# Expert rows 0 to 196 in pairs: two steps of the main program ahead of two gelus, more adds on VectorE, low parts two gathers later

## What is computed

```python
def swiglu_ffn(h, w_in, w_out):
    gate, up = jnp.split(h @ w_in, 2, axis=-1)
    return (jax.nn.silu(gate) * up) @ w_out

# PEER, for a block of 128 tokens: 8 heads x 16 experts = 128 experts for each token
experts = jnp.take_along_axis(cand_i, pos, axis=-1)
gates = jax.nn.softmax(top_s, axis=-1)
u = expert_down[experts]
vv = expert_up[experts]
act = jax.nn.gelu(jnp.einsum("thkd,td->thk", u, hb), approximate=False)
return jnp.einsum("thk,thkd->td", (gates * act), vv)
```

## Time and profile before

| | |
|---|---|
| median of three runs | 3392.49 us |
| the profiled execution, its time | 3392.38 us |
| its span on the core | 3390.6 us |
| TensorE, VectorE, ScalarE, GpSimd busy | 87%, 64%, 44%, 23% |
| DMA | 833 MB, mean 246 GB/s |
| table loads of ScalarE | 222, 284.8 us |
| gathers | 512, 536.9 MB |

### The profile page before, as it was taken

One profiled execution on the slowest core, in us unless ns is written; L12 is line 12 of the kernel. 1 busy time (PEld: TensorE's weight loads), 2 busy tenths in 40 slices (PEclk: granted clock), 3 DMA queues, 4 the chain that ended last, 5 costly groups with the idle time before them and its releaser, 6 DMA issues.

```text
span 3390.6 us, 38246 instructions
## 1 busy us (share of the span) xinstructions
PE 2964.8 (87%) x13622; PEld 2137.2 (63%) x13622; DVE 2184.4 (64%) x3979; ACT 1507.6 (44%) x2991; POOL 771.4 (23%) x629
## 2 busy tenths in 40 slices
PE   6989999899998899888979998799896777777777
PEld 5868888688776699767868786377673232223222
DVE  7655443586776576255487885877689589655555
ACT  3243222444665444572245556984333333333333
POOL 0000000000111000000027873212333444434432
PEclk8999999999998899999989999899997999999999
DMA  6544444243213387320449999776887999999997
GB/s 245 186 142 136 137 146 142 90 150 119 69 63 104 116 263 257 113 88 12 148 165 343 370 370 359 293 280 236 331 343 310 421 421 421 421 422 422 421 421 331
DMA packets 156925, 833.13 MB, mean 246 GB/s; under 512 B 17344, under 2 KB 19520, under 8 KB 91072
## 3 DMA queue, kind: packets, MB, share of 16 engines
q0 software_dynamic: 73728, 536.90, 39.5%
q1 hardware_dynamic: 79056, 286.30, 25.3%
q10 hardware_dynamic: 3952, 7.48, 0.6%
HBM read 828.52 MB, written 2.10 MB: 245 GB/s over the span
## 4 chain that ended last, share of the span: by engine, by line
PE 52%; DMA 19%; DVE 14%; ACT 9%; issue 4%; POOL 1%; DVEq 0%; SPq 0%; POOLq 0%; ACTq 0%
PE psum L153 51%; DMA tail<-in_experts,tail 19%; ACT L164 4%; DVE tail L187 3%; ACT arena L164 2%; DVE tail L170 2%; ACT tail L164 2%; DVE tail L182 1%; DVE arena L182 1%; DVE rounded L170 1%; DVE region L170 1%; DVE tail L193 1%; POOL tail L216 1%; DVE tail L190 1%; ACT region L164 1%
## 5 line engine op out<-in xcount | busy, mean ns | idle before, releaser
L153 PE MATMUL psum<-tail,arena 128*128 128x256 f32 (+2 forms) x3572 | 1266.8, 500 | 256.5 <-ACT arena L164 240.3
L153 PE MATMUL psum<-rounded,rounded 128*128 128x512 f32 (+1 forms) x7080 | 1332.0, 348 | 57.9 <-DVE rounded L182 41.0
L153 PEld LDWEIGHTS psum<-rounded,rounded 128*128 128x128 f32 x7080 | 1128.4, 191 | 245.1 <-issue 68.6
L153 PEld LDWEIGHTS psum<-tail,arena 128*128 128x128 f32 x3572 | 662.9, 197 | 779.8 <-issue 718.7
L216 POOL DMA_INDIRECT tail<-in_experts,tail x512 | 581.7, 1136 | 1395.9 <-PE psum L153 722.3
L187 DVE CUSTOM_DVE_ANT_0 tail<-tail 128x1024 f32<-128x1024 f32 x512 | 645.1, 1267 | 342.5 <-DMA tail<-in_experts,tail 339.5
L164 ACT ACTIVATE tail<-tail 128x1 f32<-128x1 f32 (+1 forms) x1056 | 267.4, 253 | 783.0 <-DVE tail L187 754.7
L164 ACT ACTIVATE rounded<-arena 128x1024 fp32r<-128x1024 f32 (+3 forms) x389 | 362.5, 949 | 383.4 <-PE psum L153 157.8
L170 DVE TENSOR_TENSOR rounded<-arena,rounded 128x1024 fp32r<-128x1024 f32 (+2 forms) x286 | 321.7, 1125 | 272.5 <-ACT rounded L164 272.2
L164 ACT ACT_TABLE_LOAD x222 | 284.8, 1283 | 14.8 <-PE psum L153 8.7
L164 ACT ACTIVATE arena<-psum 128x256 f32<-128x256 f32 (+1 forms) x210 | 97.3, 480 | 327.9 <-PE psum L153 323.8
(11 more groups left out here) (88 smaller groups left out, 1601.7 us busy)
## 6 DMA issues: line engine op xcount, KB each, us to landing
arena<-in_ada SPq DMA_DIRECT2D x136, 512.0 KB
arena<-in_fin SPq DMA_DIRECT2D x132, 512.0 KB
arena<-in_fout SPq DMA_DIRECT2D x60, 512.0 KB
arena<-in_win SPq DMA_DIRECT2D x56, 512.0 KB
arena<-in_mxbc SPq DMA_DIRECT2D x32, 512.0 KB
arena<-in_pq SPq DMA_DIRECT2D x32, 512.0 KB
arena<-in_ain SPq DMA_DIRECT2D x24, 512.0 KB
arena<-in_mz SPq DMA_DIRECT2D x16, 512.0 KB
```

Of the source, the lines that this page charges most:

```text
L153: return self.e.matmul(o, a, b, start=start, stop=stop, skip_group_check=skip)
```

## The change

Rows 0 to 195 are taken in turns of two, (0, 1), (2, 3), ..., and rows from 196 on one by one. In a turn TensorE makes the step of the first row, the add of the first row of the turn before, the step of the second and the add of the second row before. ScalarE makes both steps, then both gelus, then both diagonals; from row 196 on the gelu stands ahead of the step as before. VectorE makes both dots, then the adds of the turn before, then both steps. `own_add` takes two in three of rows 0 to 67, from row 0 on, where it took one in four from row 17 on; from row 68 to 71 it takes one in two. `pool_low` for piece n stands behind gather n + 2. For block 1 `dve_finish` comes behind the steps.

```diff
+        TOGETHER, APART = 68, 196
...
-            return 16 <= s < 124 and s % (4 if n < 72 else 2 if n < 192 else 8 if n < 256 else 16) == 1
+            if n < TOGETHER:
+                return s % 3 > 0
+            return 16 <= s < 124 and s % (2 if n < 192 else 8 if n < 256 else 16) == 1
...
-                if 3 <= n < len(HALF):
-                    pool_low(e, SPLIT[AGAIN + n])
+                if 5 <= n < len(HALF) + 2:
+                    pool_low(e, SPLIT[AGAIN + n - 2])
...
+        TURNS = [(g,) for g in range(0)]
+        TURNS += [(g, g + 1) for g in range(0, APART, 2)]
+        TURNS += [(g,) for g in range(APART, 512)]
+
         def pe_experts(e):
             main = both(pe_half(e, 1), pe_main(e, 1))
             before_rows(main, iter(()))
...
+            behind = []
+            for rows in TURNS:
+                for g in rows:
+                    c, grp = ALL_GROUPS[g]
...
+                    steps_of(c, grp, main, ranks)
+                    if grp % 2:
+                        next(late, None)
+                    for m in behind[0:1] if g < rows[-1] else behind:
+                        pe_add(e, *ALL_GROUPS[m])
+                    behind = behind[1:] if g < rows[-1] else []
+                if rows[0] and rows[0] % 128 == 0:
+                    pe_finish(e, rows[0] // 128 - 1)
+                behind = list(rows)
+            pe_add(e, *ALL_GROUPS[511])
             pe_finish(e, 3)
 
         def act_experts(e, ranks):
...
-                act_gate(e, c, grp)
-                act_diag(e, c, grp)
-                if c and grp == 8:
-                    store(e, c - 1)
-                steps_of(c, grp, main, ranks)
-                if grp % 2:
-                    next(late, None)
+            for rows in TURNS:
+                if rows[0] >= APART:
+                    act_rows(e, rows)
+                for g in rows:
...
+                    steps_of(c, grp, main, ranks)
+                    if grp % 2:
+                        next(late, None)
+                if rows[0] < APART:
+                    act_rows(e, rows)
+
+        def act_rows(e, rows):
+            for g in rows:
+                act_gate(e, *ALL_GROUPS[g])
+            for g in rows:
+                act_diag(e, *ALL_GROUPS[g])
+            c, grp = ALL_GROUPS[rows[0]]
+            if c and grp == 8:
+                store(e, c - 1)
 
         def dve_experts(e, ranks):
...
-                dve_dots(e, c, grp)
-                if g:
-                    dve_add(e, *ALL_GROUPS[g - 1])
-                if c and grp == 1:
-                    dve_finish(e, c - 1)
-                steps_of(c, grp, main, ranks)
...
+            behind = ()
+            for rows in TURNS:
+                for g in rows:
+                    dve_dots(e, *ALL_GROUPS[g])
+                for g in behind:
+                    dve_add(e, *ALL_GROUPS[g])
+                for g in rows:
...
+                    if c > 1 and grp == 1:
+                        dve_finish(e, c - 1)
+                    steps_of(c, grp, main, ranks)
+                    if grp % 2:
+                        next(late, None)
+                    if c == 1 and grp == 1:
+                        dve_finish(e, c - 1)
+                behind = rows
+            dve_add(e, *ALL_GROUPS[511])
             dve_finish(e, 3)
```

## The result

The changed kernel takes 3442.8 us (median of 4 runs, 3438.8 to 3447.3) against 3392.1 us before: ratio 1.0149, 95% interval 1.0131 to 1.0166. It is 50 us **slower**; the forecast was 3382. The profiled execution took 3438.8 us, its span is 3436.9.

The account below looks back on a forecast made before the run. TensorE was taken to bound rows 0 to 65, ScalarE attention, VectorE 2472 to 2602 us, and DMA the rest. Terms -4 + 0 - 3 - 2 + 3 - 4 = -10 us took 3392.4 to 3382 us, range 3352 to 3408.

Parts of the forecast that it names:

- VectorE at 280: Rows 0 to 65: the bound changes from TensorE at 284 us to VectorE at 280, -4 us, bounds -9 to +20.
- The third rival: Rows 0 to 65: VectorE becomes the bound, later than TensorE was; stretch 300.5 us (+16.5), total 3407; chance 0.19.
- the first rival: Rows from 2071 to 2602 us: pairs free two thirds of TensorE's idle time, 38 us, total 3354; chance 0.12.
- My upper bound, half a microsecond for 33 pairs: Rows 0 to 65: later low parts cost 0, at most half a microsecond per pair, +16 us.
- The condition I wrote: Rows 0 to 65: 3.4 to 4.6 us of TensorE work against 1.4 + 2.1 us for gather and low part.
- low parts that hold TensorE: A sign that the prediction is wrong: low parts hold TensorE; no size given.
- +3 with +7 as the bound: Attention: pairs cost +3 us, between +1.6 by the walk and +7 as upper bound; the other end -8.
- my walk: Attention: a pair's chain of dots, gelus, add, heads and exponential sums to 8.8 us, against 8.6 for two rows before.
- -3 taken: Projections and 2198 to 2382 us, full of TensorE work: pairs gain 3 of 13.7 us of TensorE's idle time.
- -4 taken: 2472 to 2602 us: two rows apart removes part of VectorE's 10.6 us of waits, -4 us, bounds 0 and -10.6.
- passed on whole to the end: The -10 us gained ahead of 2602 us reaches the end whole, since everything behind is one DMA stream.
- the fourth rival: Slots run short: pairs hold more rows and gathers start later; 3409 us, or 3400 with fewer; chance 0.12.

Follow-up runs that it names:

- pairs_0_196: Kernel before with only the pairs for rows 0 to 195, own_add and the low parts' place unchanged: 3436.2 us, ratio 1.0123.
- a_own_old: Changed kernel with own_add of before (13 of the first 66 rows on VectorE instead of 44): 3438.6 us, ratio 1.0133.
- pairs_68_196: Kernel before with pairs for rows 68 to 195 alone, all else as before: 3414.5 us, ratio 1.0063.
- best1: Kernel before with pairs for rows 108 to 143 alone and low parts two gathers later, own_add as before: 3381.9 us, ratio 0.9966.
- b_own_new: Kernel before with only more adds on VectorE (rows n % 3 > 0 of the first 68): 3413.2 us, ratio 1.0062.
- a_low0: Changed kernel with the low part of piece n right behind gather n again: 3434.9 us, ratio 1.0124.
- pairs_gelu_first: As pairs_0_196, but in a turn ScalarE makes both gelus and both diagonals ahead of both steps: 3427.7 us, ratio 1.0101.

## Why the prediction was wrong

**Pairs in rows 0 to 65: the step that failed.** The sum has no term for them. I costed the adds and the low parts in that stretch, and the pairs only from row 66 on; TensorE was the bound, and I took it that an order which adds no instruction could not cost it anything. Alone they cost +26 us in the stretch, 310 instead of 284 (22 by the difference of the two times). The mechanism that I had to see is that ScalarE, idle 44% of that stretch, stands in a ring: gelus now stand behind a high part that waits for TensorE's step (148.8 us of waits instead of 18.2) and TensorE's adds behind the gelus (21.7 us instead of 3.8). The last link, gathers behind the adds, shows only once the low parts come later: GpSimd waits 6.2 us for TensorE's adds in pairs_0_196 and 95.5 in a_own_old. Each of the two changes of place alone moved the wait from one member to the next and gave 0 and 3 us; both at once took back 16 of the 26. The cause of the other 10 stays open.

**Adds on VectorE: right mechanism, wrong size, and on the wrong side.** "VectorE at 280" should have been 305. The price of one moved add is (69.3 - 15.8) / 31 = 1.73 us, above my upper bound of 1.558; the dots rose as well, 1558 to 1641 ns, and VectorE's busy time by 62 us where I had 44.5. 290.1 busy, 7.8 of landing waits and my 7.1 between instructions make 305, which is the stretch. The third rival (300.5) was the right one in place and mechanism for this part and near in price. It had 0.19; with 1.5% of room left, more was due. My own terms end at 300.5, +16.5, where I wrote +20 as the upper end; and the first rival's 3354 stands in my range as 3352.

**Low parts: 0 was right alone and wrong in company.** Alone 283 us, no difference. With both other parts TensorE waits 54.9 us for them. My upper bound, half a microsecond for 33 pairs, was 16 us; putting them back in the changed kernel gave 8 us. The condition I wrote, 3.4 to 4.6 us of TensorE between the add of n - 4 and step n, holds for adds of TensorE only. The add of row n - 4 is now VectorE's in two of three, and GpSimd waited 47.3 us for those. I had named low parts that hold TensorE as a sign of being wrong.

**Attention: the right waits, each too small.** I took +3 with +7 as the bound, and growth by over 7 us as a sign of being wrong: it is +10.7 in the changed kernel and +13.5 in pairs_68_196 (85.1 us for rows 92 to 107). A pair takes 10.3 us where my walk gave 8.8; two rows took 8.95 before, not 8.6. Of the 30 table loads of rows 92 to 107 15 did go (ScalarE 67.60 to 45.45 us), and bought nothing. VectorE's busy time stayed, 60.48 and 60.77 us, so the growth is its waiting. The wait for the exponential is not new, as I had it; the one for the gelus is. VectorE's waits in the kernel before, 2130.8 to 2202.4 us, and its two longest in the changed kernel, 2161.9 to 2244.2:

```profile
DVE tail L202 <- ACT tail L165: 9.4, 8, 1.6
```

```profile
DVE tail L202 <- ACT tail L165: 11.6, 8, 2.1
DVE tail L182 <- ACT tail L164: 5.8, 7, 1.4
```

Waits for landings (1.4 us), for TensorE (0.8) and 0.3 more make 19.9 against 9.4. Two pairs of the changed kernel on VectorE (start us, us, and in brackets the idle time before):

```profile
2185.68 1.28 DVE L182 SCALAR_TENSOR_TENSOR tail<-tail 128x1024 f32<-128x1024 f32 x1 [0.69 <-ACT tail L164]
...
2189.63 0.16 DVE L202 RECIPROCAL tail<-tail 128x1 f32<-128x1 f32 x1 [0.77 <-ACT tail L165]
...
2190.72 0.35 DVE L177 TENSOR_SCALAR tail<-psum,tail 128x128 f32<-128x128 f32 x1 [0.47 <-PE psum L158]
...
2195.56 1.28 DVE L182 SCALAR_TENSOR_TENSOR tail<-tail 128x1024 f32<-128x1024 f32 x1 [1.03 <-ACT tail L164]
...
2200.20 0.16 DVE L202 RECIPROCAL tail<-tail 128x1 f32<-128x1 f32 x1 [1.45 <-ACT tail L165]
```

In the first the add waits 0.69 us for the gelus (0.5 forecast) and the normalisation 0.77 for the exponential (0.9); in the second 1.03 and 1.45. The mean of the eight pairs is 0.73 and 1.45. The wait of 0.47 us for the scores of the second step is TensorE's, and I had left it out.

**Stretches full of TensorE: too timid.** -3 taken; rows 108 to 143 are -10.5 in the changed kernel and -9 in best1, with the projections (rows 76 to 91) at 61.7 us instead of 59.8.

**Query, gap and catching up: wrong sign.** -4 taken for 2472 to 2602; measured +3.8 for rows 172 to 189, -0.4 for rows 190 to 195, and +8 behind. My "passed on whole to the end" missed that pairs also decide how soon the DMA stream is full once the light rows begin. The slots, which I named as the fourth rival, may be part of that: one slot is 14 us. How much of the pairs' loss is slots and how much is order wasn't separated.

Together: 21 (adds) + 44 (pairs) - 2 (low parts, no difference that can be told) would be 63; the whole change costs 50. In rows 0 to 65, which adds and pairs both hold up, they cost 21 and 26 us alone and 34 together.

## What to carry to other kernels

An order that adds no work can cost as much as added work, when engines that look idle are links of a ring: write the ring down (who waits for whom, over how many rows) before giving a reordering the price zero, and do it in the very stretch where the bound engine is full. Moving work from an engine at 98% to one at 80% is worth at most what the second has free, counted with the prices of the moment at which both run; here the 31 adds cost 1.73 us each, not the 1.43 read while there were 11 of them. Freeing an engine's time gains nothing where a chain through its neighbour gets longer: in attention ScalarE lost 22 us of work and the stretch grew. The pairs gained 9 us on 36 of 196 rows and lost more on the others. And a change of order also moves the marks by which stretches are cut: cut where both kernels have finished the same work.

## What I had not expected of the hardware

TensorE's steps themselves became slower. The 65 steps' loads took 211.4 us busy against 193.9, 17.5 us more for the same loads, at a granted clock of 0.92 instead of 1.00. A step behind a wait, on TensorE in the changed kernel, and the next one:

```profile
1899.56 5.43 PE L153 MATMUL psum<-rounded,rounded 128*128 128x256 f32 x24 [4.55 <-POOL rounded L170]
...
1899.72 5.03 PEld L153 LDWEIGHTS psum<-rounded,rounded 128*128 128x128 f32 x23
...
1906.55 2.83 PEld L153 LDWEIGHTS psum<-rounded,rounded 128*128 128x128 f32 x23 [0.24 <-issue]
```

The windows of the two steps, with the granted clock third from the end:

```profile
1899.70:1904.80 5.10, 5.10 (x24) 5.10 (x25) 4.93 (x7) 0.00 (x0) 2.93 (x2) 0.50 1.00 379
...
1906.50:1909.50 3.00, 3.00 (x25) 2.83 (x23) 2.91 (x9) 0.00 (x0) 2.51 (x2) 1.00 0.28 76
```

After 4.55 us without work the 23 loads took 5.03 us, near twice the 2.83 us of the next step, at a granted clock of 0.50 against 1.00: the lower of the clock's two levels, 1.2 instead of 2.4 GHz. This wait cost TensorE 2.2 us more than its own length.

VectorE's 128x1024 adds, which have two inputs in SBUF, lasted 1650 ns (b_own_new), 1737 (changed kernel) and 1997 (a_low0) beside GpSimd's low parts, and 1281 ns in attention, where there are none. The Trainium skill, "SBUF — State Buffer", section "Who interferes with whom", has the two exclude each other for a whole instruction. The traces agree, and show that it goes by who starts first. In rows 0 to 65 of all traces an add that meets no low part, or starts ahead of the one that it meets, lasts 1273 to 1283 ns in the mean; the one exception, 3.10 us in pairs_0_196, starts 0.02 us ahead. An add that starts while a low part runs ends 1.08 to 1.09 us behind that low part, in every trace. There are 9 of 42 such adds in b_own_new, 3016 ns in the mean; 16 of 41 in the changed kernel, 2451 ns; 17 of 41 in a_low0, 3011 ns; and none in pairs_gelu_first. A low part and an add of the changed kernel that starts 0.24 us behind it:

```profile
1792.97 2.17 POOL L170 TENSOR_TENSOR rounded<-arena,rounded 128x1024 fp32r<-128x1024 f32 x1
...
1793.21 3.01 DVE L182 SCALAR_TENSOR_TENSOR tail<-tail 128x1024 f32<-128x1024 f32 x1
```

So the price of a moved add hangs on whether its start falls into a low part, and a change of order moves that too: the same 11 adds take 1277 ns each in pairs_gelu_first and 1758 in pairs_0_196.
